# A two-block transformer kernel: one scale step moved from GpSimd to VectorE, and small shifts in three hand-written step tables

## What is computed

```python
# first block, differential attention: queries and keys are normed per 64 columns
qd = rms_norm(q_d.reshape(B, S, 8, 2, 64), diff_q_norm_g)
kd = rms_norm(k_d.reshape(B, S, 8, 2, 64), diff_k_norm_g)
o_d = diff_attention(qd, kd, v_d, lam)          # 8 heads, causal, ALiBi

# second block, latent attention: keys are made from a small latent
kv = (rmsnorm(c_kv, kv_c_gain) @ w_ukv).reshape(B, S, 8, 64 + 64)
k_nope = rmsnorm(kv[..., :64], kn_gain)         # normed per head
k_rope = rope(rmsnorm(k_rope_in, kr_gain), cos, sin)
s = (q_nope @ k_nope.T + q_rope @ k_rope.T) * scale
```

## Time and profile before

| what | value |
|---|---|
| median of three runs | 896.99 us (896.86 to 897.04) |
| the profiled execution, its own time | 896.86 us |
| its span in the profile | 895.0 us |
| outside of the span | 1.9 us |
| granted TensorE clock, mean | 1.000 |
| PE busy | 888.5 us, 99% of the span |
| DVE, ACT, POOL busy | 435.9, 413.8, 442.9 us |

### The profile page before, as it was taken

How to read it: one execution, slowest core, us unless ns; L and a number is a source line. 1 busy time by engine, 2 the same in 40 slices (tenths; PEclk the granted TensorE clock), 3 DMA queues, 4 the chain that set the end, 5 groups by cost and what they waited for, 6 DMA issues and landing times.

```text
span 895.0 us, 12730 instructions
## 1 busy us (share of the span) xinstructions
PE 888.5 (99%) x4648; PEld 724.8 (81%) x4648; DVE 435.9 (49%) x938; ACT 413.8 (46%) x912; POOL 442.9 (49%) x396
## 2 busy tenths in 40 slices
PE   9999999999999999999999999999999999999998
PEld 7878888888888888888888888889888767777776
DVE  3221242445111346686876455646647875543731
ACT  5533323334223454656665444244535685655531
POOL 5544446435447565467333345544548474234362
PEclk9999999999999999999999999999999999999999
DMA  8533222323233443444434233233354322111113
GB/s 315 160 84 94 71 72 71 95 71 118 94 94 95 142 119 94 118 118 103 133 95 119 72 133 125 95 107 97 98 103 116 111 74 69 31 42 48 48 49 117
DMA packets 54830, 89.70 MB, mean 100 GB/s; under 512 B 5440, under 2 KB 23616, under 8 KB 54768
## 3 DMA queue, kind: packets, MB, share of 16 engines
q1 hardware_dynamic: 53280, 88.34, 32.9%
q10 hardware_dynamic: 1488, 0.55, 0.3%
HBM read 78.36 MB, written 2.12 MB: 90 GB/s over the span
## 4 chain that ended last, share of the span: by engine, by line
PE 96%; DVE 2%; ACT 1%; DMA 0%; issue 0%; SPq 0%; DVEq 0%; ACTq 0%
PE Z L1869 26%; PE Z L1871 26%; PE Z L1870 26%; PE A L2056 3%; PE A L2065 2%; PE A L2094 2%; PE A L1988 2%; PE A L2039 1%; PE A L1977 1%; PE A L1976 1%; PE A L1879 1%; PE A L2001 1%; PE A L1930 1%; PE A L1957 1%; DMA sgd_sb<-in_xT 0%; PE A L1909 0%
## 5 line engine op out<-in xcount | busy, mean ns | idle before, releaser
L1032 POOL TENSOR_TENSOR w_lo<-raw,w_hi 128x512 fp32r<-128x512 f32 (+1 forms) x262 | 348.0, 1335 | 426.1 <-ACT w_hi L638 425.2
L638 ACT CAST w_hi<-raw 128x512 fp32r<-128x512 f32 (+1 forms) x262 | 158.4, 615 | 291.3 <-PE Z L1871 260.9
L1869 PE MATMUL Z<-w_hi,hT_hi 128*128 128x512 f32 (+1 forms) x544 | 217.3, 400 | 0.0
L1871 PE MATMUL Z<-w_hi,hT_lo 128*128 128x512 f32 (+1 forms) x544 | 211.6, 389 | 0.0
L1870 PE MATMUL Z<-w_lo,hT_hi 128*128 128x512 f32 (+1 forms) x544 | 211.0, 388 | 0.0
L1869 PEld LDWEIGHTS Z<-w_hi,hT_hi 128*128 128x128 f32 x544 | 102.4, 188 | 20.9 <-issue 2.1
L1871 PEld LDWEIGHTS Z<-w_hi,hT_lo 128*128 128x128 f32 x544 | 102.1, 188 | 20.7
L1870 PEld LDWEIGHTS Z<-w_lo,hT_hi 128*128 128x128 f32 x544 | 102.5, 188 | 17.6
L1869 PE MATMUL Z<-hT_hi,w_hi 128*128 128x512 f32 x260 | 112.7, 434 | 0.8 <-DVE hT_lo L1302 0.4
L1871 PE MATMUL Z<-hT_hi,w_lo 128*128 128x512 f32 x260 | 102.2, 393 | 0.0
L1870 PE MATMUL Z<-hT_lo,w_hi 128*128 128x512 f32 x260 | 101.7, 391 | 0.0
(11 more groups left out here) (263 smaller groups left out, 1341.6 us busy)
## 6 DMA issues: line engine op xcount, KB each, us to landing
raw<-in_w_in SPq DMA_DIRECT2D x59, 512.0 KB, 3.6
raw<-in_w_in SPq DMA_DIRECT2D x66, 256.0 KB, 3.1
k_stack<-keys_once SPq DMA_DIRECT2D x32, 256.0 KB, 4.6
raw<-in_w_out SPq DMA_DIRECT2D x16, 512.0 KB, 3.6
raw<-in_ret_w_o SPq DMA_DIRECT2D x8, 512.0 KB, 3.3
raw<-in_diff_w_o SPq DMA_DIRECT2D x8, 512.0 KB, 3.2
x_sb<-in_x SPq DMA_DIRECT2D x4, 512.0 KB, 5.6
x_sb<-in_xT SPq DMA_DIRECT2D x4, 512.0 KB, 6.3
```

The lines of the kernel that those rows point to most:

```text
L638: act.copy(w_hi[:, s % SPLIT_SLOTS, 0:width], raw[:, c % RAW_SLOTS, s - CHUNK_START[c], 0:width]).then_inc(hi_ready, 1)
L1032: pool.tensor_tensor(w_lo[:, s % SPLIT_SLOTS, 0:width], raw[:, c % RAW_SLOTS, s - CHUNK_START[c], 0:width], w_hi[:, s % SPLIT_SLOTS, 0:wid ...
L1869: pe.matmul(out, l_hi, r_hi, start=first, stop=False)
L1871: return pe.matmul(out, l_lo, r_hi, start=False, stop=last)
```

## The change

Four tables get other numbers, and the four multiplications of the latent keys go from POOL to DVE.

```diff
-DIFF_STEPS = ((52, 0), (91, 9), (96, 9), (106, 11), (158, 31), (198, 49), (252, 76), (257, 76), (273, 86))
+DIFF_STEPS = ((52, 0), (91, 9), (96, 9), (102, 11), (158, 31), (198, 49), (252, 76), (257, 76), (273, 86))
...
-FIRST_ROOTS = {7: (0,), 8: (1,), 9: (2,)}
-EARLY_SCALES = {24: (0, 0), 26: (0, 1), 32: (0, 2), 33: (0, 3), 88: (1, 0), 97: (1, 1), 99: (1, 2), 101: (1, 3)}
+FIRST_ROOTS = {7: (0,), 9: (1,), 10: (2,)}
+EARLY_SCALES = {26: (0, 0), 27: (0, 1), 32: (0, 2), 33: (0, 3), 86: (1, 0), 87: (1, 1), 88: (1, 2), 97: (1, 3)}
...
-LATENT_PIECES = (23, 25, 27, 29, 31, 33, 35, 37, 39, 46, 47, 49, 50)
-KEY_SCALES = {51 + t: t for t in range(4)}
+LATENT_PIECES = (23, 25, 27, 29, 31, 33, 35, 37, 39, 46, 47, 49, 50, 52, 53, 55, 56)
...
-            def latent_keys(t):
-
-                k4 = z_sb[:, t, Z_KCAT:Z_KCAT + 768].rearrange("p (h e) -> p h e", h=H)
-                kv4 = m_sb[:, t, :].rearrange("p (h e) -> p h e", h=H)
-                if t == 0:
-                    pool.wait_ge(key_roots, 1)
-                pool.tensor_tensor(k4[:, :, 0:NOPE], kv4[:, :, 0:NOPE],
-                                   rstd[:, 64 + 8 * t:72 + 8 * t].unsqueeze(2).broadcast_to([P, H, NOPE]),
-                                   ALU.mult).then_inc(keys_scaled, 1)
...
                 for part in range(4):
                     rsqrt(32, (part,), 64)
-                    if part == 3:
-                        dve.engine_nop().then_inc(key_roots, 1)
+                    yield
+                dve.wait_ge(rope_spread, TT)
+                for t in range(TT):
+                    link(dve.tensor_tensor(k4[:, t, :, 0:NOPE], kv4[:, t, :, 0:NOPE],
+                                           rstd[:, 64 + 8 * t:72 + 8 * t].unsqueeze(2).broadcast_to([P, H, NOPE]), ALU.mult))
                     yield
...
-                if (p, c) == (H // 2, 1):
-                    pe.wait_ge(rope_spread, TT)
-                    pe.wait_ge(keys_scaled, TT)
```

More of the change, by code:

```diff
@@ L385, in build @@
         gated, head_normed, roots_ready = sem("gated"), sem("head_normed"), sem("roots_ready")
-        rope_spread, key_roots, keys_scaled = sem("rope_spread"), sem("key_roots"), sem("keys_scaled")
+        rope_spread = sem("rope_spread")
         r_t, r_turned, r_s, r_u, r_i = (sem(n) for n in ("r_t", "r_turned", "r_s", "r_u", "r_i"))
@@ L1174, in heads_slot @@
                         latent_queries(ROTATIONS[v + t])
-                    if v + t in KEY_SCALES:
-                        latent_keys(KEY_SCALES[v + t])
             def diff_roots(part):
@@ L1762, in _ @@
             k4 = z_sb[:, :, Z_KCAT:Z_KCAT + 768].rearrange("p t (h e) -> p t h e", h=H)
+            kv4 = m_sb[:, :, :].rearrange("p t (h e) -> p t h e", h=H)
             def latent_sums(q):
```

## The result

The changed kernel takes **904.54 us** (median of four runs, 903.22 to 904.95) against 897.0 (896.86 to 897.04) for the kernel before: a ratio of 1.0082, 95% interval 1.0064 to 1.0099. It is slower, as forecast, but the time lies 2.0 us above the predicted 902.5 and 0.5 above the top of the range, 904.0.

The account below looks back on a forecast made before the run. PE, 99% busy, was taken to bound the kernel, so time goes only where PE waits. 0.96 + 2.63 + 1.95 = 5.5 us on a median of 896.99 gave 902.5 us, range 898.8 to 904.0.

Parts of the forecast that it names:

- What bounds the kernel: Whole span: PE is 99% busy, so time can go only where PE waits; a better schedule gives back at most 0.4 us.
- Turns of DVE and POOL: DVE's two-input scales and POOL's instructions exclude each other: 0.55 us for a scale, 1.15 for a subtraction.
- rival of no turns: No turns, or only at one of three places: 2.3 us in all, 899.3 us; chance 0.20.
- Place A: Roots and scales of pair 0: a POOL subtraction ahead of the roots makes PE start tile 32 late, cost 0.96 us.
- Place B: Scales of pair 1: two more scales ahead of the row maxima make PE start tile 96 late, cost 2.63 us.
- the spare ahead of tile 96: PE took tile 96 at 342.94 after the emptying ended at 342.78, with 0.10 us to spare.
- Place C: Latent keys: four scales moved from POOL to DVE make two PE transposes late, 0.47 and 1.48 us, together 1.95.
- The steps: Steps 10 to 28 of DIFF_STEPS come up to four tiles earlier; nothing waited there, cost zero.
- POOL's gain at C: Latent keys: four POOL instructions of 1.04 us go, but nobody is named as waiting for them: gain zero.
- Span and 1.9 outside: The profiled execution of 896.86 us is a span of 895.0 plus 1.9 us outside it.
- The clock: Rival: the 2.6 us pause ahead of tile 96 lowers PE's clock; two us of it give 904.5 us; chance 0.05.
- Its clock stay at 1.00: Sign in the changed profile: PE's clock stays at 1.00, the upper of its two levels.

Follow-up runs that it names:

- narrow scales: The changed kernel with the second and third scale of pair 1 cut to 2 of every 64 columns, order and count of instructions kept: 900.54 us.
- A alone: The kernel before with only the roots of pair 0 moved to 7, 9, 10 and its first two scales to 26 and 27: 897.84 us.
- B alone: The kernel before with three scales of pair 1 at tiles 86, 87, 88, the fourth at 97, and the DIFF_STEPS step moved from 106 to 102: 900.68 us.
- four scales ahead: The changed kernel with all four scales of pair 1 ahead of the row maxima (tiles 86 to 89): 905.16 to 906.06, then 904.40 to 905.10 us.

## Why the prediction was right or wrong

- **What bounds the kernel**: right. PE's waits were the place to look, and 5.55 of the 5.7 us in the span are in them.
- **Turns of DVE and POOL**: right, and shown by the narrow scales. The rival of no turns (0.20) is out; its sum of 2.3 us is less than half of what came in the span.
- **Place A**: 0.96 forecast, 0.98 measured. **Place B**: 2.63 and 2.68; the subtraction did take its turn between the second and the third scale. The 0.06 us between a release and PE's start, an estimate, was too little here: behind an emptying it is 0.14, so the spare ahead of tile 96 was about 0.02 us and not 0.10, which is about the 0.05 by which B came out dearer. **Place C**: 0.47 + 1.48 and 0.45 + 1.44. **The steps**: zero, and zero.
- **POOL's gain at C**: zero, as said; PE's pauses at C are the same to 0.01 us with and without nops in the four places.
- **"Span and 1.9 outside"**: wrong by 0.4. The prediction carried the time outside the span over unchanged. The 1.9 became 2.3, about 0.3 of it with C's control; no run here shows where the other 0.1 comes from, since A alone and B alone leave it at 1.8. By itself this term would not have mattered: with it the sum is 902.9, inside the range, and the runs at full clock took 902.98 and 903.22.
- **The clock, the step that failed**: the prediction had the mechanism as a rival, for a pause of this length at this place, and even "two us of it give 904.5 us", within 0.1 us of the median. That nearness is luck: the 2 us were a guess for the clock alone, and what came is some 1.5 from the clock and 0.4 from outside the span. The prediction gave this rival 0.05 and left it outside the range, where three runs of five show it. The range as written does not follow from its own bounds either: they end at 2.3 and 6.8 us, 899.3 and 903.8, and 904.0 lies beyond the upper one, not "most of the way" to it; 904.54 lies beyond both. The reason it gave for the 0.05, "no pause in the middle of the work to compare", argues for ignorance, not for a small chance: nothing in the profile bore on which way it would go. With a chance of a half the range would have had to reach over it.
- **"Its clock stay at 1.00"**, as a sign to look for in the changed profile, held for that one execution and not for the kernel: a profile is one run of two sorts.

Two executions of one kernel, four scales ahead, have the fall of the clock 1.1 us behind PE's restart and 0.4 us ahead of it. The Trainium skill, TensorE: Matmul & The Clock Gate, Part 1, says that a monitor sets PE's clock by how busy PE has been recently. It also says that the number of slowed matmuls at a kernel's start varies between runs of one kernel. The traces agree with the first; the variation they show is of a fall in the middle of the work, after a pause.

## What to carry to other kernels

Before you put one more two-input DVE instruction ahead of something that PE waits for, look at what POOL has lined up: each one can cost a whole instruction of POOL besides its own 0.6 us; the price of two more was 2.7 us, where their own work is 1.2. Price a pause of PE twice: once for its length, and once for the clock behind it (here some 1.1 to 1.8 us where it fell once, the spread of the runs included: in 13 of 20 runs with a pause of 2.7 us, in all 8 with 3.3, in none up to 1.84); give that its own line in the sum, and when no row bears on it let the range reach over it. If a pause of that length can't be avoided, harmless matmuls in it can be worth more than nothing; here they went into a bank that was being filled anyway and changed the result by next to nothing.

## What the runs showed of the hardware that was not expected

- The granted clock falls to 0.50 after a pause of PE of 2.7 us, for 3.4 us each time it was seen, and begins at different distances from the pause: at 436.5 (0.5 us ahead of the restart), 346.6 (0.4 ahead) and 348.6 (1.1 behind). Only what of it meets work costs, half its length.
- Twelve matmuls of no use in the pause took 1.0 to 1.7 us off the median (904.54 and 903.85 without them, 902.85 with).
- A DVE instruction of 16 columns took 580 ns beside POOL's single-input line 1106 and 165 ns when it got in between.
- With four scales moved, the time outside the span was 1.82 us with the nops and semaphore waits kept and 2.10 with them taken out, 0.3 us more.
